# Moving the causal convolution and the gated input of a recurrent stage between three engines

## The chip, the cores and the metric

The kernel runs on one core of a Trainium2 chip. A core has a matrix engine (TensorE, PE in the rows), VectorE (DVE), ScalarE (ACT), GpSimd (POOL) and SyncE (SP), which here issues most of the DMA transfers. Each engine works through its own instruction stream in order; semaphores tie the streams together. The metric is the device time of one launch in microseconds; lower is better.

## The reference, cut to what matters

One step of a two-layer decoder: layer 0 is sparse attention, layer 1 a recurrent block (RG-LRU), and each is followed by a gated channel mixer. 256 prompt tokens and 8 sample tokens go through together, so a matrix multiply has 264 columns. The change lies in the recurrent block only:

```
gate, xb = split(a @ w_in)                       # 1024 channels each
xc = b + sum(xp[:, k:k + t] * w[k] for k in 0..3)  # xp: 3 kept rows, then xb
r  = sigmoid(block_diag(xc, w_ga) + b_ga)
ig = sigmoid(block_diag(xc, w_gx) + b_gx)
log_a = -8 * r * softplus(-lam);  a_t = exp(log_a)
b_t = sqrt(-expm1(2 * log_a)) * ig * xc
h_t = a_t * h_{t-1} + b_t                        # scan over the 256 tokens
y = (gelu(gate) * h) @ w_out
```

## The kernel before, in words

Activations are kept with channels on the 128 partitions and tokens along the free dimension, so 1024 channels are 8 chunks of 128x264. A matrix product is made of "units": 128 output channels, each from 8 chunks times three float16 matmuls (high times high, low activation times high, high times low weight; lines 1467, 1470, 1473). `hi` (ScalarE, line 595) and `lo` (VectorE, line 971) split a unit's weights into the two halves ahead of use.

The recurrent stage has 16 units, U_XB to U_XB+15: eight of `xb`, then eight of the gate branch. TensorE runs them in order and, after unit n+3, the two float32 gate products of chunk n (line 1797), for which it waits for the finished convolution `xc` (`xc_full`) and for the tanh of chunk n-2. Then it runs 20 small matmuls on ones (line 1479), and after that the first four output units together, chunk by chunk (lines 1614 to 1616), where each chunk c waits for the low half of y (`y_lo`, line 1376). All order is written out by hand in the loops over i = 0..15 that every engine has. In the kernel before, a chunk n of the stage takes these steps:

- VectorE, i = n: `xb` = result x reciprocal norm (line 1386; line 1388 for the gate branch). It waits for the TensorE unit.
- ScalarE: `tap3` = xb x w0 into a buffer of its own (line 923).
- GpSimd: the copy of the last rows of xb (line 1949), `xc` = xb x w3 + bias (line 1950), the sample columns' kept part `rpre` (line 1952), and `xc` += tap3 shifted by three (line 1954), which posts `xc_part`.
- VectorE, i = n+1 (`taps`): the shifts by one and by two (lines 1342 and 1345), then `xc_full`; then a `lo`.
- TensorE: gate products. ScalarE, i = n+4 (`keep_gates`): two tanh (line 841), a tanh and an exp (lines 844 and 846); it waits until the gated input of chunk n-2 has freed the buffer (`ix_done`).
- GpSimd, i = n+4: gated input `ix` = (tanh + 1) x xc, as an add (line 1959) and a product (line 1960), which posts `ix_done`.
- VectorE, i = n+5 (`b_part`): ix = (... + 1) x ix (line 1352).
- ScalarE takes the square root of four chunks at once (line 930, after chunks 3 and 7), GpSimd multiplies it in (`whole_b`, line 1943), VectorE scans (line 1362), GpSimd multiplies the Gelu by a row factor (line 1968), VectorE makes y (`mix`, line 1372), ScalarE its high half (lines 939 and 944), VectorE its low half (`mix_rest`, line 1376).

On GpSimd the loop interleaves `whole_b(n)` with the row factor of chunk n-4; on VectorE `scan(6)` and `scan(7)` stand after the low half of chunk 2.

Of the kernel before, what the change touches and what calls it, by code (L numbers as in the profile page):

```python
# [27 lines left out]
TP = 256  # L28
# [154 lines left out]
def build(nc, a, o):  # L183
    with ExitStack() as ctx:
# [148 lines left out]
        tap3 = z32  # L333
# [78 lines left out]
        tap3_done, xc_part, xc_full = sem("tap3_done"), sem("xc_part"), sem("xc_full")  # L412
# [169 lines left out]
        def _(act):  # L582
# [328 lines left out]
            for i in range(2 * DC):  # L911
# [7 lines left out]
                if i < DC:  # L919
                    act.wait_ge(acc_read, before(u) + 1)  # L920
                    if i >= 2:
                        act.wait_ge(xc_part, i - 1)
                    nc.scalar.activation(tap3[:, i % 2, :], xb[:, i % 2, :], ACT.Copy,
                                         scale=prm[:, ROW_CONV_W, i:i + 1]).then_inc(tap3_done, 1)
# [37 lines left out]
        def _(dve):  # L962
# [377 lines left out]
            def taps(n):  # L1340
                dve.wait_ge(xc_part, n + 1)
                steps.done(v.scalar_tensor_tensor(xc[:, n, 1:TP], xb[:, n % 2, 0:TP - 1], prm[:, ROW_CONV_W + 2, n:n + 1],
                                                  xc[:, n, 1:TP], ALU.mult, ALU.add))
                steps.wait()
                v.scalar_tensor_tensor(xc[:, n, 2:TP], xb[:, n % 2, 0:TP - 2], prm[:, ROW_CONV_W + 1, n:n + 1],
                                       xc[:, n, 2:TP], ALU.mult, ALU.add).then_inc(xc_full, 1)

            def b_part(n):

                dve.wait_ge(gate_ab, 2 * n + 2)  # L1350
# [27 lines left out]
            for i in range(2 * DC):  # L1378
# [4 lines left out]
                if i < DC:  # L1383
                    if i >= 2:
                        dve.wait_ge(xc_full, i - 1)
                    v.tensor_tensor(xb[:, i % 2, :], acc[:, u % 4, 0:T], rinv[:], ALU.mult).then_inc(acc_read, 1)
# [8 lines left out]
                if i >= 10:  # L1395
                    scan(i - 10)
                if i >= 14:
# [3 lines left out]
            for n in range(2, DC):  # L1401
                if n == 4:
                    scan(6)
                    scan(7)
# [410 lines left out]
        def _(pool):  # L1815
# [51 lines left out]
            def conv_params():  # L1867
# [4 lines left out]
                for k in range(3):  # L1872
                    w = prm[:, ROW_CONV_W + k:ROW_CONV_W + k + 1, :].to_broadcast([P, NS, DC])
                    small(g.tensor_tensor(rpre[:] if k == 0 else part, state[:, :, k, :], w, ALU.mult))
                    if k:
                        small(g.tensor_tensor(rpre[:], rpre[:], part, ALU.add))

# [67 lines left out]
            for i in range(DC + 4):  # L1945
                if i < DC:
# [3 lines left out]
                    small(g.tensor_scalar(xc[:, i, :], xb[:, p, :], prm[:, ROW_CONV_W + 3, i:i + 1],  # L1950
                                          prm[:, ROW_CONV_B, i:i + 1], ALU.mult, ALU.add))
                    small(g.tensor_tensor(xc[:, i, TP:T], xc[:, i, TP:T], rpre[:, :, i], ALU.add))
# [79 lines left out]
```

## Time and profile before

| what | us |
|---|---|
| median of 3 runs | 615.56 (615.41 to 616.15) |
| the profiled execution, its own time | 615.82 |
| its span, first to last instruction | 614.0 |
| TensorE busy in the span | 590.7 (96%) |
| VectorE, ScalarE, GpSimd busy | 457.2, 367.0, 238.6 |

The recurrent stage reaches from about 335 us to 405 us of the span. Times in the rows further down are microseconds from the start of the span; "idle before" is followed by the instruction that ended the idle time.

### The profile page before, as it was taken

To read this page: it belongs to the slowest core of one execution; us is meant where nothing else is said; L and a number is where in the kernel's file an instruction comes from. 1 tells how busy PE (TensorE), PEld (TensorE's weight loads), DVE (VectorE), ACT (ScalarE), POOL (GpSimd) and SP (SyncE) were. 2 spreads that over 40 slices of the span, in tenths; PEclk is the share of its full clock that TensorE was granted. 3 is DMA by queue.
4 is the path that set the end of the run, shared out by engine and by line. 5 is a ranking of instruction groups with operands and counts; after the bars stand their busy time and mean duration, and the time that the engine had idled before them with its cause. 6 is when DMAs were issued, how large, how long until landed. Compare 5 with 4: busy or idle time off the path is not lost.

```text
span 614.0 us, 12864 instructions
## 1 busy us (share of the span) xinstructions
PE 590.7 (96%) x5069; PEld 508.5 (83%) x5069; DVE 457.2 (74%) x897; ACT 367.0 (60%) x623; POOL 238.6 (39%) x259
## 2 busy tenths in 40 slices
PE   7899998999999999999999999798999999999995
PEld 7788886978888888888888778686888888888885
DVE  4788999456797778888677785978877777875432
ACT  6974556576666566565555688556656656653322
POOL 4232337733255445450000697823445545420000
PEclk9999998999999999999999999998999999999998
DMA  9949587319676667688996851054666666878501
GB/s 263 263 114 242 154 240 232 113 57 292 216 217 201 192 193 201 193 239 242 269 261 185 215 160 36 1 170 140 195 188 202 197 187 201 236 223 224 150 6 70
DMA packets 205421, 113.29 MB, mean 185 GB/s; under 512 B 5561, under 2 KB 202217, under 8 KB 205337
## 3 DMA queue, kind: packets, MB, share of 16 engines
q1 hardware_dynamic: 203169, 106.33, 61.4%
q0 software_dynamic: 1680, 5.79, 2.8%
q8 instruction: 40, 0.66, 0.4%
q10 hardware_dynamic: 512, 0.35, 0.2%
q14 instruction: 20, 0.16, 0.1%
HBM read 108.83 MB, written 3.86 MB: 184 GB/s over the span
## 4 chain that ended last, share of the span: by engine, by line
PE 70%; DVE 15%; POOL 6%; ACT 5%; issue 3%; DMA 1%; DVEq 0%; POOLq 0%; ACTq 0%
PE acc L1467 20%; PE acc L1470 20%; PE acc L1473 20%; DVE w_lo L971 5%; ACT w_hi L595 2%; POOL area L1954 1%; DVE area L1096 1%; PE acc L1614 1%; PE acc L1479 1%; DMA stage<-in_w_ffn_down 1%; PE acc L1616 1%; PE acc L1615 1%; POOL area L1950 1%; POOL area L1959 1%; POOL rtail L1949 1%
## 5 line engine op out<-in xcount | busy, mean ns | idle before, releaser
L1467 PE MATMUL acc<-aH,w_hi 128*128 128x264 f16 (+1 forms) x904 | 250.7, 277 | 1.7 <-DVE aL L980 1.6
L1470 PE MATMUL acc<-aL,w_hi 128*128 128x264 f16 (+1 forms) x904 | 250.6, 277 | 0.0
L1473 PE MATMUL acc<-aH,w_lo 128*128 128x264 f16 (+1 forms) x904 | 250.4, 277 | 0.0
L971 DVE SCALAR_TENSOR_TENSOR w_lo<-stage,w_hi 128x1024 f16<-128x1024 f32 (+1 forms) x155 | 204.0, 1320 | 33.6 <-ACT w_hi L595 33.2
L595 ACT ACTIVATE w_hi<-stage 128x1024 f16<-128x1024 f32 (+1 forms) x155 | 171.4, 1109 | 34.0 <-PE acc L1473 27.5
L1467 PE MATMUL acc<-zH,w_hi 128*128 128x264 f16 x384 | 106.0, 276 | 0.0
L1470 PE MATMUL acc<-zL,w_hi 128*128 128x264 f16 x384 | 106.0, 276 | 0.0
L1473 PE MATMUL acc<-zH,w_lo 128*128 128x264 f16 x384 | 106.0, 276 | 0.0
L1467 PEld LDWEIGHTS acc<-aH,w_hi 128*128 128x128 f16 (+1 forms) x904 | 89.0, 98 | 16.6 <-DVE aL L980 2.2
L1470 PEld LDWEIGHTS acc<-aL,w_hi 128*128 128x128 f16 (+1 forms) x904 | 90.3, 100 | 14.2 <-issue 0.3
L1473 PEld LDWEIGHTS acc<-aH,w_lo 128*128 128x128 f16 (+1 forms) x904 | 90.3, 100 | 13.3
L1899 POOL TENSOR_TENSOR scratch<-work,r0z 128x264 f32<-128x264 f32 x44 | 65.5, 1489 | 81.3 <-ACT work L865 81.3
L1897 POOL COPY ftail<-scratch 128x10 f32<-128x10 f32 x44 | 46.9, 1066 | 37.1 <-DVE scratch L1286 37.0
L860 ACT ACTIVATE work<-scratch,fprm 128x264 f32<-128x264 f32 x44 | 26.7, 607 | 54.1 <-DVE scratch L1286 54.0
L1286 DVE TENSOR_TENSOR scratch<-acc,rinv 128x264 f32<-128x264 f32 x44 | 19.0, 432 | 41.9 <-PE acc L1473 41.8
L1467 PEld LDWEIGHTS acc<-zH,w_hi 128*128 128x128 f16 x384 | 37.6, 98 | 5.7
L1473 PEld LDWEIGHTS acc<-zH,w_lo 128*128 128x128 f16 x384 | 37.6, 98 | 5.6
L1470 PEld LDWEIGHTS acc<-zL,w_hi 128*128 128x128 f16 x384 | 37.6, 98 | 5.5
L1833 POOL TENSOR_TENSOR sqsum<-sqsum,sq 128x264 f32<-128x264 f32 x21 | 16.5, 785 | 62.6 <-ACT sq L611 62.2
L865 ACT ACTIVATE work<-work 128x264 f32<-128x264 f32 x44 | 18.6, 423 | 35.0 <-DVE work L1297 34.9
L1910 POOL TENSOR_TENSOR area<-area,scratch 128x264 f32<-128x264 f32 x16 | 18.6, 1164 | 40.1 <-DVE area L1053 40.0
L604 ACT ACTIVATE aH<-hT,gcol 128x264 f16<-128x264 f32 x24 | 12.3, 514 | 32.5 <-DVE hT L1316 18.5
(407 smaller groups left out, 963.5 us busy)
## 6 DMA issues: line engine op xcount, KB each, us to landing
stage<-in_w_ffn_up SPq DMA_DIRECT2D x88, 512.0 KB, 4.0
stage<-in_w_ffn_down SPq DMA_DIRECT2D x32, 704.0 KB, 5.6
stage<-in_w_attn_in SPq DMA_DIRECT2D x22, 512.0 KB, 5.9
stage<-in_w_rec_in SPq DMA_DIRECT2D x16, 512.0 KB, 4.9
stage<-in_w_attn_out SPq DMA_DIRECT2D x8, 512.0 KB, 3.7
stage<-in_w_rec_out SPq DMA_DIRECT2D x8, 512.0 KB, 3.7
area<-in_w_attn_in SPq DMA_DIRECT2D x4, 512.0 KB, 5.5
area<-in_x_prompt SPq DMA_DIRECT2D x2, 512.0 KB, 4.8
```

Source lines behind the costliest of these rows:

```text
L595: nc.scalar.activation(halves_of(u)[0], stage[:, s, 0:n, 0:cols], ACT.Copy, scale=WSCALE).then_inc(hi_done, 1)
L860: nc.scalar.activation(c32[:, p, :], gs[:, p, :], ACT.Identity, scale=fprm[layer][:, FROW_W + 2, j:j + 1], bias=fprm[layer][:, FROW_B, j:j ...
L865: nc.scalar.activation(c32[:, p, :], c32[:, p, :], ACT.Gelu_apprx_tanh).then_inc(gelu_done, 1)
L971: v.scalar_tensor_tensor(low, stage[:, place_in_line(u) % 4, 0:n, 0:cols], WSCALE, high, ALU.mult, ALU.subtract).then_inc(lo_done, 1)
L1286: v.tensor_tensor(gs[:, p, :], acc[:, u % 4, 0:T], rinv[:], ALU.mult).then_inc(acc_read, 1)
L1467: t_.matmul(out, high[:, c, :], xH[:, x0 + c, :], start=first and c == 0, stop=False)
L1470: t_.matmul(out, high[:, c, :], xL[:, x0 + c, :], start=False, stop=False)
L1473: ins = t_.matmul(out, low[:, c, :], xH[:, x0 + c, :], start=False, stop=last and c == n - 1)
L1833: g.tensor_tensor(sqsum[:], sqsum[:], sq[:, c % 2, :], ALU.add).then_inc(ss_done, 1)
L1897: g.tensor_copy(ftail[:, :, j], gs[:, p, TP - 2:T]).then_inc(tail_copied, 1)
L1899: g.tensor_tensor(gr[:, p, :], c32[:, p, :], r0z[:], ALU.mult).then_inc(gr_done, 1)
L1910: g.tensor_tensor(dst, dst, rot[0:part, (before(u) + 1) % 2, :], ALU.subtract).then_inc(roped, 1)
```

## The change

The first convolution term goes to ScalarE: it writes xb x w3 + bias straight into `xc`, and the buffer `tap3` goes. VectorE makes all three shifted taps (shifts 1, 2 and 3) and the small add of the sample columns, and it also makes the gated input, in one instruction instead of two, at the head of `b_part`. GpSimd keeps the copy of the last rows, `whole_b` and the row factor. Before VectorE overwrites an xb buffer it now also waits for the GpSimd copy from it (`rt_copied`). Two orders change: all `whole_b` now come before all row factors on GpSimd, and on VectorE the scans 4 to 7 stand two and two in the last two rounds, ahead of the first and second `mix`. The file's line numbers move by a few.

```diff
-                    if i >= 2:
-                        act.wait_ge(xc_part, i - 1)
-                    nc.scalar.activation(tap3[:, i % 2, :], xb[:, i % 2, :], ACT.Copy,
-                                         scale=prm[:, ROW_CONV_W, i:i + 1]).then_inc(tap3_done, 1)
+                    nc.scalar.activation(xc[:, i, :], xb[:, i % 2, :], ACT.Identity, scale=prm[:, ROW_CONV_W + 3, i:i + 1],
+                                         bias=prm[:, ROW_CONV_B, i:i + 1]).then_inc(xc_part, 1)
...
             def taps(n):
                 dve.wait_ge(xc_part, n + 1)
-                steps.done(v.scalar_tensor_tensor(xc[:, n, 1:TP], xb[:, n % 2, 0:TP - 1], prm[:, ROW_CONV_W + 2, n:n + 1],
-                                                  xc[:, n, 1:TP], ALU.mult, ALU.add))
-                steps.wait()
-                v.scalar_tensor_tensor(xc[:, n, 2:TP], xb[:, n % 2, 0:TP - 2], prm[:, ROW_CONV_W + 1, n:n + 1],
-                                       xc[:, n, 2:TP], ALU.mult, ALU.add).then_inc(xc_full, 1)
+                if n == 0:
+                    dve.wait_ge(pre_done, 3)
+                for back in (1, 2):
+                    steps.done(v.scalar_tensor_tensor(xc[:, n, back:TP], xb[:, n % 2, 0:TP - back],
+                                                      prm[:, ROW_CONV_W + 3 - back, n:n + 1], xc[:, n, back:TP], ALU.mult, ALU.add))
+                    if back == 1:
+                        v.tensor_tensor(xc[:, n, TP:T], xc[:, n, TP:T], rpre[:, :, n], ALU.add)
+                    steps.wait()
+                v.scalar_tensor_tensor(xc[:, n, 3:TP], xb[:, n % 2, 0:TP - 3], prm[:, ROW_CONV_W, n:n + 1],
+                                       xc[:, n, 3:TP], ALU.mult, ALU.add).then_inc(xc_full, 1)
 
             def b_part(n):
 
+                dve.wait_ge(gate_tanh, 2 * n + 2)
+                v.scalar_tensor_tensor(ix[:, n, :], gates[:, n % 2, 1, :], 1.0, xc[:, n, :], ALU.add, ALU.mult).then_inc(ix_done, 1)
...
                     if i >= 2:
                         dve.wait_ge(xc_full, i - 1)
+                        dve.wait_ge(rt_copied, i - 1)
...
-                if i >= 10:
+                if 10 <= i < 14:
                     scan(i - 10)
+                if i >= 14:
+                    scan(2 * i - 24)
+                    scan(2 * i - 23)
...
             for n in range(2, DC):
-                if n == 4:
-                    scan(6)
-                    scan(7)
                 mix(n)
...
                     g.tensor_copy(rtail[:, :, i], xb[:, p, TP - 3:T]).then_inc(rt_copied, 1)
-                    small(g.tensor_scalar(xc[:, i, :], xb[:, p, :], prm[:, ROW_CONV_W + 3, i:i + 1],
-                                          prm[:, ROW_CONV_B, i:i + 1], ALU.mult, ALU.add))
-                    small(g.tensor_tensor(xc[:, i, TP:T], xc[:, i, TP:T], rpre[:, :, i], ALU.add))
-                    pool.wait_ge(tap3_done, i + 1)
-                    g.tensor_tensor(xc[:, i, 3:TP], xc[:, i, 3:TP], tap3[:, p, 0:TP - 3], ALU.add).then_inc(xc_part, 1)
-                if i >= 4:
-                    n = i - 4
-                    pool.wait_ge(gate_tanh, 2 * n + 2)
-                    pool.wait_ge(xc_full, n + 1)
-                    small(g.tensor_scalar(gates[:, n % 2, 1, :], gates[:, n % 2, 1, :], 1.0, None, ALU.add))
-                    g.tensor_tensor(ix[:, n, :], gates[:, n % 2, 1, :], xc[:, n, :], ALU.mult).then_inc(ix_done, 1)
                 if i >= 9:
                     whole_b(i - 9)
-            for n in range(3, DC + 4):
-                if n < DC:
-                    whole_b(n)
-                if n >= 4:
-                    pool.wait_ge(ggelu, 1 if n < 8 else 2 if n < 11 else 3)
-                    g.tensor_tensor(gateT[:, n - 4, :], gateT[:, n - 4, :], r0T[:], ALU.mult).then_inc(gr0_done, 1)
+            for n in range(3, DC):
+                whole_b(n)
+            for n in range(DC):
+                pool.wait_ge(ggelu, 1 if n < 4 else 2 if n < 7 else 3)
+                g.tensor_tensor(gateT[:, n, :], gateT[:, n, :], r0T[:], ALU.mult).then_inc(gr0_done, 1)
```

VectorE's row in the middle of the stage (i = 6), before; `area` holds xb, xc, ix and the gates, `prm` the weights, `ca` a unit's low weights:

```order
L1386 TENSOR_TENSOR area<-acc,rinv 128x264
L1342 SCALAR_TENSOR_TENSOR area<-area,prm 128x255
L1345 SCALAR_TENSOR_TENSOR area<-area,prm 128x254
L971 SCALAR_TENSOR_TENSOR ca<-stage,ca 128x1024
L1352 SCALAR_TENSOR_TENSOR area<-area 128x264
```

The same round in the changed kernel:

```order
L1391 TENSOR_TENSOR area<-acc,rinv 128x264
L1342 SCALAR_TENSOR_TENSOR area<-area,prm 128x255
L1345 TENSOR_TENSOR area<-area,rpre 128x8
L1342 SCALAR_TENSOR_TENSOR area<-area,prm 128x254
L1347 SCALAR_TENSOR_TENSOR area<-area,prm 128x253
L968 SCALAR_TENSOR_TENSOR ca<-stage,ca 128x1024
L1353 SCALAR_TENSOR_TENSOR area<-area 128x264
L1356 SCALAR_TENSOR_TENSOR area<-area 128x264
```

The round grows by three instructions: the small add, the tap by three, and the gated input.

GpSimd's last part of the stage before, where `area<-area` without r0T is `whole_b` or the gated input, and r0T is the row factor:

```order
L1959 TENSOR_SCALAR area<-area 128x264
L1960 TENSOR_TENSOR area<-area 128x264
L1943 TENSOR_TENSOR area<-area 128x264 x3
L1968 TENSOR_TENSOR area<-area,r0T 128x264
L1943 TENSOR_TENSOR area<-area 128x264
L1968 TENSOR_TENSOR area<-area,r0T 128x264
L1943 TENSOR_TENSOR area<-area 128x264
L1968 TENSOR_TENSOR area<-area,r0T 128x264
L1943 TENSOR_TENSOR area<-area 128x264
L1968 TENSOR_TENSOR area<-area,r0T 128x264 x5
```

And all that GpSimd does between the two sums of squares in the changed kernel:

```order
L1838 TENSOR_TENSOR sqsum<-sqsum,sq 128x264 x7
L1955 COPY rtail<-area 128x11 x8
L1949 TENSOR_TENSOR area<-area 128x264 x8
L1962 TENSOR_TENSOR area<-area,r0T 128x264 x8
L1964 COPY htail<-area 128x8x9
```

The eight `whole_b` now stand in a row ahead of the eight row factors, and the five instructions per chunk of convolution and gated input are gone.

## Rows read from the trace of the kernel before

**Rows 1.** The page, busy time (share of the span) and instructions of each engine.

```profile
PE 590.7 (96%) x5069; PEld 508.5 (83%) x5069; DVE 457.2 (74%) x897; ACT 367.0 (60%) x623; POOL 238.6 (39%) x259
```

**Rows 2.** Waits of TensorE, 342 to 405: total us, times, longest.

```profile
PE acc L1614 <- DVE zL L1376: 3.5, 4, 1.9
PE misc L1797 <- DVE area L1345: 0.7, 1, 0.7
```

**Rows 3.** Timeline of TensorE, 386 to 400: start, length, instruction, idle before it.

```profile
388.49 2.39 PE L1479 MATMUL misc<-ones 128*128 128x128 f32 x20
392.74 0.29 PE L1614 MATMUL acc<-zH 128*128 128x264 f16 x1 [1.85 <-DVE zL L1376]
...
398.99 0.29 PE L1614 MATMUL acc<-zH 128*128 128x264 f16 x1 [1.15 <-DVE zL L1376]
```

**Rows 4.** Timeline of VectorE, 355 to 368, same columns.

```profile
355.51 1.22 DVE L971 SCALAR_TENSOR_TENSOR zL<-stage,zH 128x1024 f16<-128x1024 f32 x1
356.65 0.42 DVE L1386 TENSOR_TENSOR area<-acc,rinv 128x264 f32<-128x264 f32 x1
...
360.35 0.42 DVE L1386 TENSOR_TENSOR area<-acc,rinv 128x264 f32<-128x264 f32 x1
361.89 0.62 DVE L1342 SCALAR_TENSOR_TENSOR area<-area,prm 128x255 f32<-128x255 f32 x1 [1.12 <-POOL area L1954]
362.55 0.48 DVE L1345 SCALAR_TENSOR_TENSOR area<-area,prm 128x254 f32<-128x254 f32 x1
...
365.00 0.42 DVE L1386 TENSOR_TENSOR area<-acc,rinv 128x264 f32<-128x264 f32 x1
```

**Rows 5.** Timeline of GpSimd, the gated input in the same stretch.

```profile
361.83 0.87 POOL L1959 TENSOR_SCALAR area<-area 128x264 f32<-128x264 f32 x1
362.79 0.86 POOL L1960 TENSOR_TENSOR area<-area 128x264 f32<-128x264 f32 x1
```

**Rows 6.** Timeline of VectorE in the channel mixer, 443 to 444.5.

```profile
442.92 0.48 DVE L1293 SCALAR_TENSOR_TENSOR work<-scratch,fprm,work 128x255 f32<-128x255 f32 x1
443.32 0.17 DVE L1295 TENSOR_TENSOR work<-work,fpre 128x8 f32<-128x8 f32 x1
443.44 0.48 DVE L1297 SCALAR_TENSOR_TENSOR work<-scratch,fprm,work 128x254 f32<-128x254 f32 x1
443.84 0.43 DVE L1272 TENSOR_TENSOR work<-acc,scratch 128x264 f32<-128x264 f32 x1
```

**Rows 7.** Timeline of ScalarE, 372 to 390.

```profile
373.01 0.85 ACT L841 ACTIVATE area<-misc,spl 128x264 f32<-128x264 f32 x2 [2.80 <-POOL area L1960]
...
383.43 1.08 ACT L930 ACTIVATE area<-area 128x1056 f32<-128x1056 f32 x1
```

**Rows 8.** Timeline of VectorE, 384 to 398.5.

```profile
387.84 1.15 DVE L1362 TENSOR_TENSOR_SCAN area<-area 128x256 f32<-128x256 f32 x1
...
394.39 0.97 DVE L1372 TENSOR_TENSOR work<-area 128x264 f32<-128x264 f32 x1
...
396.18 1.81 DVE L1362 TENSOR_TENSOR_SCAN area<-area 128x256 f32<-128x256 f32 x2
...
398.11 0.43 DVE L1372 TENSOR_TENSOR work<-area 128x264 f32<-128x264 f32 x1
```

**Rows 9.** Timeline of GpSimd, 384 to 398.5.

```profile
386.99 0.74 POOL L1968 TENSOR_TENSOR area<-area,r0T 128x264 f32<-128x264 f32 x1 [0.57 <-ACT area L933]
...
392.36 4.50 POOL L1968 TENSOR_TENSOR area<-area,r0T 128x264 f32<-128x264 f32 x5
```

**Rows 10.** Stretches: length, TensorE busy (instructions), granted clock, DMA share, GB/s.

```profile
375.00:385.00 10.00, 10.00 (x90) 1.00 0.01 2
390.00:394.00 4.00, 2.15 (x20) 1.00 0.00 0
418.00:422.00 4.00, 2.06 (x17) 1.00 0.57 167
422.00:426.00 4.00, 3.52 (x14) 0.57 0.61 177
```

More of the change, by code:

```diff
@@ L332, in build @@
         xb = area1[:, 7392:7392 + 2 * T].rearrange("p (b t) -> p b t", b=2)
-        tap3 = z32
         wordsH = zH[:, DC:FC, :].rearrange("p c t -> p (c t)")
@@ L411, in build @@
             sem(n) for n in ("lg_mm", "lg_max", "p_exp", "p_rcp", "p_norm", "p_turned", "p_kept", "o_mm", "o_hi", "o_lo"))
-        tap3_done, xc_part, xc_full = sem("tap3_done"), sem("xc_part"), sem("xc_full")
+        xc_part, xc_full = sem("xc_part"), sem("xc_full")
         gate_mm, gate_tanh, gate_ab, ix_done, bq_done, b_root, b_full, hs_done = (
@@ L1874, in conv_params @@
                     small(g.tensor_tensor(rpre[:] if k == 0 else part, state[:, :, k, :], w, ALU.mult))
-                    if k:
+                    if k == 1:
                         small(g.tensor_tensor(rpre[:], rpre[:], part, ALU.add))
+                g.tensor_tensor(rpre[:], rpre[:], part, ALU.add).then_inc(pre_done, 1)
             def ffn_params(layer):
```

## The prediction

> **What bounds the kernel now.** I read the page first, then TensorE's waits, then the timelines of the recurrent stage. TensorE is busy for 590.7 of 614.0 us [rows 1], so a change to the other engines can only win back TensorE's idle time, and here only that of the recurrent stage. The list of its waits there is short [rows 2]: 3.5 us in four waits for the low half of y, and 0.7 us in one wait for the convolution. The timeline shows where the 3.5 us sit [rows 3]. The sixteen units end at 388.49, twenty small matmuls follow, and the first matmul on y starts only at 392.74, after 1.85 us of idle time. The fourth y chunk starts at 398.99, again after waiting 1.15 us; between them stand two idle times of about 0.3. A y chunk is 12 matmuls; at 90 in 10.00 us [rows 10] that is 1.35 us of work, yet four chunks' starts lie 6.25 us apart instead of 4.05. From 398.99 on nothing waits. So **the start of the fourth y chunk sets the end**, and whatever moves it moves all that follows.
>
> What feeds y? In the middle of the stage VectorE's results come 4.65 us apart, 360.35 and 365.00 [rows 4], and within a round VectorE stands idle for 1.12 us until GpSimd's part of the convolution is there. GpSimd also makes the gated input in two instructions of 0.87 and 0.86 us [rows 5], and ScalarE's gates of chunk 5 start at 373.01 after waiting 2.80 us for it [rows 7]. The chain is thus: GpSimd, then ScalarE's gates and roots up to 384.51, then GpSimd's and VectorE's last steps, then TensorE.
>
> **Part 1, the middle of the stage.** GpSimd loses five instructions a chunk and keeps a copy; nobody waits for it there any more. VectorE's round becomes longer in work and loses its wait. The nearest rows for its new taps are those of the channel mixer, which has the same pattern without GpSimd beside it [rows 6]: the first tap takes 0.40 from start to start, the small add 0.12, a tap 0.40. Here the second tap is followed by one that waits for it, and such a handover costs 0.04 after the end instead of 0.08 before it (361.89 plus 0.62, next at 362.55 [rows 4]), so 0.52. Together 0.40 + 0.12 + 0.52 + 0.40 = 1.44. The result's own multiplication is 0.42 long [rows 4]; less the 0.08 by which neighbours overlap that is 0.35 from start to start. The weight split takes 1.14 (355.51 to 356.65). The gated input and the `b_part` after it are two more of 0.42 with a handover between: 0.35 + 0.52 = 0.87. A round is 0.35 + 1.44 + 1.14 + 0.87 = 3.80 us in place of 4.65.
>
> Result 5 comes at 356.65 now; up to there the new round has no gated input (2.93 us), which is TensorE's own pace or a little more, so I leave that time as it is. Result 8 is then at 356.65 + 3 x 3.80 = 368.05, and the gated input of chunk 3, for which ScalarE's gates of chunk 5 wait, is ready at 368.05 + 0.35 + 1.44 + 0.45 = 370.3. **That is 2.7 us before 373.01.** ScalarE's first term is an activation of the same size as the one it replaces and stays off this chain. Its queue behind is the same as before, so the second root ends 11.50 us after the gates of chunk 5 start (373.01 to 384.51 [rows 7]): 381.8. The new wait for GpSimd's copy costs nothing, since GpSimd has nothing queued ahead of it; behind it on VectorE stand all taps, and if the cover were gone, each round would grow by what the copy is late. TensorE's 0.7 us wait for the convolution mostly goes, though the gates' tanh then is next to be late; I count 0.5, so the sixteen units end at 388.0 and the fifteenth at 388.0 - 24 x 0.111 = 385.3.
>
> **Part 2, the end of the stage.** GpSimd has four `whole_b` and then the first row factor: five instructions of 0.74 alone and 0.90 (4.50 for five) against a busy VectorE [rows 9]. The first row factor is there between 385.5 and 386.3; before it was at 387.73. So it is no longer late, and **VectorE's own queue is next**. After the fifteenth unit it holds the result (0.35), a small product (0.4, an estimate from the 0.43 of the larger `mix`), scans 4 and 5, a `mix`, the last result, scans 6 and 7, a small add (0.2), a `mix` and the first low half. Against GpSimd a scan takes 1.07 from start to start (1.15 long), a `mix` 0.90 (0.97 long), where alone it takes 0.43; the pair of scans at the very end takes 1.74 (1.81) [rows 8]. All at the slow price: 385.3 + 0.35 + 0.4 + 2.14 + 0.9 + 0.35 + 1.74 + 0.2 + 0.9 + 0.9 = 393.2 for the first y chunk, 1.8 more, 395.0, for the second. But GpSimd's row factors 4 to 7 wait for a Gelu that stands behind the first y on ScalarE, so GpSimd rests for about 1 us, just while VectorE scans; and it is through by 394. That takes 0.4 to 0.8 off: the second y chunk starts at about 394.5. From there a chunk costs TensorE 1.35 and VectorE 0.9 to 1.8, once 0.1 late at most, and no scan stands in between any more. The fourth y chunk starts at 394.5 + 2.7 + 0.1 = 397.3 instead of 398.99.
>
> **The sum:** 398.99 - 397.3 = 1.7 us earlier. Against the profiled execution of 615.82 us (span 614.0) this is 614.1; the median of the runs shown, 615.56, lies 0.26 lower, so I forecast **613.9 us**. From here on 0.2%, or 1.2 us, is what a measurement can tell from no change: "faster" means below 614.3, "slower" above 616.8.
>
> **The bounds.** If GpSimd never got in VectorE's way, each of the nine contended steps would save 0.5, but TensorE's small matmuls (388.0 plus 2.39) hold the first chunk at 390.4 and the fourth at 394.5: 4.5 us earlier. That would need GpSimd to be done before 386, which the Gelu forbids; half of the way, 2.9 us, is the most I believe, 612.7. The other bound is the tap: among the taps of before are some of 0.62 instead of 0.48 [rows 4]. Three such a round make 0.45 more.
>
> **Rivals.** *VectorE becomes the pacing engine and the stage gets slower.* Its place is the rounds 0 to 7, its price what a round takes beyond 3.80. With all three taps at 0.62 and the GpSimd copy getting in between for 0.2, a round is 4.45, and the rounds before the fifth grow as well: result 8 comes 8 x 0.65 = 5.2 later, at 373.2, the gated input of chunk 3 2.4 us after 373.01, and with the new order giving back about 0.7 at the end the fourth chunk is 1.7 late: 617.3. It decides from a round of about 4.2 us on. For it speaks that VectorE gets all the work of a queue that is already 3.5 us long; against it that the slow taps stand beside a GpSimd instruction, and the same taps of the channel mixer are 0.48 throughout.
>
> *The end is given back to contention.* VectorE waits out each GpSimd instruction in full: 0.35 + 0.74 = 1.09 a step instead of 0.90, over nine steps 1.7 us, so 615.6: the gain is gone. The rows show 0.90 for VectorE and 0.90 for GpSimd in the same stretch [rows 8, 9], which is less than 1.09, so that only a part is blocked. The Trainium skill has such a rule on its page "SBUF — State Buffer", in "SBUF: two separate sides": a VectorE instruction with two SBUF inputs and a GpSimd instruction that reads SBUF share one port pair, and the one that comes second is blocked until the first is finished altogether. By that rule the time would be this rival's, 615.6; the trace here agrees that they block each other and does not agree on the whole length.
>
> *The clock falls at the joint.* From 418 to 422 TensorE was busy for 2.06 of 4 us, and in the next 4 us the mean granted clock was 0.57, mostly the lower level, 1.2 GHz, in place of 2.4; it ran 14 instructions where 36 fit [rows 10]; by the clock's share, 0.43 of 4 us, 1.7 us were lost. From 390 to 394 it was busy for 2.15 of 4 us and the clock stayed. In the changed kernel its idle time before y is in one piece, 390.4 to 393. If the clock falls there, 1.7 to 2 us go: 615.8. The opposite is as open: that the dip after 422, which no step of this sum touches, is not there after the shift, giving 612.2.
>
> **Chances and range.** The forecast 0.50, spread from 612.7 to 615.1, of which 0.36 lies below 614.3; the missing dip or a deeper gain 0.10; contention in full 0.13; the clock at the joint 0.14; VectorE as pacing engine 0.13. Faster is 0.36 + 0.10 = 0.46, within 0.2% is 0.14 + 0.13 + 0.14 = 0.41, slower 0.13. The range takes in the dip at 612.2 and goes up to 616.9, which leaves out most of the slow rival. TensorE does the same work in all cases, and no DMA is moved.
>
> **What would show it.** VectorE's results in rounds 5 to 8 3.8 us apart, with no idle time behind GpSimd; taps of 0.48; ScalarE's gates of chunk 5 at 370 and the second root ending at 382; the first row factor done by 386.5; the first y chunk at 392.6 to 393.2, only one long idle time on TensorE before it, and the fourth near 397.3. I would be wrong first in the round: if it is over 4.2 us, there is no gain. Second in the queue after the fifteenth unit: if the first y chunk starts after 394.3, the order of the scans has eaten what the middle won.

## The result and the profile after

| what | before, us | changed, us |
|---|---|---|
| median of 8 runs each, side by side | 615.31 (613.17 to 616.15) | 610.93 (610.26 to 612.69) |
| profiled execution, its own time | 615.82 | 612.69 |
| its span | 614.0 | 610.6 |

The ratio, estimated from all executions of both, is 0.9945, 95% interval 0.9931 to 0.9959: by it the changed kernel is 3.4 us faster, where 1.7 was forecast. (The two medians lie 4.4 apart and the two means 3.6; eight executions of each leave that much open.) The median of 610.93 is outside the range of 612.2 to 616.9. The sign was right, the size was not.

The lines of the changed kernel that answer to those of before follow. The page, busy time, for [rows 1]; GpSimd gave up 31 us and VectorE took 2:

```profile
PE 588.4 (96%) x5069; PEld 508.0 (83%) x5069; DVE 459.5 (75%) x921; ACT 367.8 (60%) x623; POOL 207.2 (34%) x219
```

Waits of TensorE between 342 and 405 for [rows 2]; the wait of 0.7 on the convolution is gone, and so is one of 0.19 on the tanh (its row stands further down), and of four on y one is left:

```profile
PE acc L1619 <- DVE zL L1380: 2.1, 1, 2.1
```

Timeline of TensorE (start, length, instruction, idle before) for [rows 3]:

```profile
386.99 2.39 PE L1484 MATMUL misc<-ones 128*128 128x128 f32 x20
391.52 0.40 PE L1619 MATMUL acc<-zH 128*128 128x264 f16 x1 [2.14 <-DVE zL L1380]
```

Timeline of VectorE in the rounds, for [rows 4] and [rows 6]. Results (L1391, L1393) come 3.79 us apart, 359.32, 363.11, 366.90, with no idle time in between, and the three taps are 0.47 or 0.48 long, none 0.62 (the first and the third of one round stand here):

```profile
359.32 0.42 DVE L1391 TENSOR_TENSOR area<-acc,rinv 128x264 f32<-128x264 f32 x1
359.66 0.47 DVE L1342 SCALAR_TENSOR_TENSOR area<-area,prm 128x255 f32<-128x255 f32 x1
...
360.69 0.48 DVE L1347 SCALAR_TENSOR_TENSOR area<-area,prm 128x253 f32<-128x253 f32 x1
...
363.11 0.43 DVE L1391 TENSOR_TENSOR area<-acc,rinv 128x264 f32<-128x264 f32 x1
```

```profile
369.19 0.85 ACT L840 ACTIVATE area<-misc,spl 128x264 f32<-128x264 f32 x2 [0.81 <-DVE area L1353]
...
379.62 1.09 ACT L927 ACTIVATE area<-area 128x1056 f32<-128x1056 f32 x1
```

The last two are ScalarE's gates of chunk 5 and its second root, for [rows 7].

The end of the stage, VectorE (for [rows 8]) and then GpSimd (for [rows 9]):

```profile
384.49 0.43 DVE L1393 TENSOR_TENSOR area<-acc,rinv 128x264 f32<-128x264 f32 x1 [1.08 <-PE acc L1478]
384.84 0.70 DVE L1365 TENSOR_TENSOR rtmp<-area,prm 128x32 f32<-128x32 f32 x1
385.57 2.23 DVE L1366 TENSOR_TENSOR_SCAN area<-area 128x256 f32<-128x256 f32 x2
387.72 0.40 DVE L1376 TENSOR_TENSOR work<-area 128x264 f32<-128x264 f32 x1
...
388.39 1.26 DVE L1366 TENSOR_TENSOR_SCAN area<-area 128x256 f32<-128x256 f32 x2
...
390.15 0.42 DVE L1376 TENSOR_TENSOR work<-area 128x264 f32<-128x264 f32 x1
390.50 0.97 DVE L1380 TENSOR_TENSOR zL<-work,zH 128x264 f16<-128x264 f32 x1
```

```profile
380.78 3.28 POOL L1949 TENSOR_TENSOR area<-area 128x264 f32<-128x264 f32 x4 [3.85 <-ACT area L927]
384.02 3.23 POOL L1962 TENSOR_TENSOR area<-area,r0T 128x264 f32<-128x264 f32 x4
389.41 3.54 POOL L1962 TENSOR_TENSOR area<-area,r0T 128x264 f32<-128x264 f32 x4 [2.16 <-ACT area L934]
```

Stretches of TensorE (length, busy and instructions, granted clock, DMA share, GB/s) for [rows 10]. The clock falls to the lower level, 1.2 GHz, right after the idle time before y; the dip that before has from 422 to 426 is not there:

```profile
390.00:392.00 2.00, 0.48 (x3) 0.88 0.00 0
392.00:394.00 2.00, 2.00 (x11) 0.50 0.04 8
394.00:396.00 2.00, 2.00 (x16) 0.76 0.00 0
...
424.00:428.00 4.00, 4.00 (x38) 1.00 0.70 202
```

Such dips have to be kept apart from the change. Over a whole execution the mean granted clock is 0.997 in the best ones, and each dip takes 0.003 of it: the profiled execution of before was at 0.991, that of the changed kernel at 0.994. One dip costs 1.7 to 1.8 us in whole executions: on the chip where the changed kernel was run a second time, 11 executions of before at 0.996 to 0.998 took 613.4 on average and 19 at 0.994 or 0.995 took 615.2. (A dip is a stretch of about 4 us in which the granted clock falls to its lower level; an execution without one, at 0.996 or above, is called undipped.) At equal clock that chip gives:

| mean granted clock | before (executions) | changed (executions) | difference |
|---|---|---|---|
| 0.996 to 0.998 | 613.4 (11) | 610.75 (5) | -2.7 |
| 0.994 to 0.995 | 615.2 (19) | 612.4 (6) | -2.8 |

**The change itself is worth about 2.75 us.** The rest of the 3.4 is then which executions fell into which group; the clocks of the first eight executions of before are not known, so for that first comparison this is an inference.

### The profile page after: what moved, and what is told of

Same layout as the page of the kernel before. It is cut to its first block, busy times and chain, and to the rows that moved or that the text cites. A ratio compares the mean times of both kernels' runs of the same rounds, so it can differ in the third digit from the quotient of the medians.

```text
span 610.6 us, 12826 instructions
## 1 busy us (share of the span) xinstructions
PE 588.4 (96%) x5069; PEld 508.0 (83%) x5069; DVE 459.5 (75%) x921; ACT 367.8 (60%) x623; POOL 207.2 (34%) x219
## 4 chain that ended last, share of the span: by engine, by line
PE 74%; DVE 15%; ACT 3%; issue 3%; DMA 2%; POOL 2%; DVEq 0%; POOLq 0%; ACTq 0%
PE acc L1472 21%; PE acc L1475 21%; PE acc L1478 21%; DVE w_lo L968 6%; DMA stage<-in_w_ffn_down 2%; ACT w_hi L594 2%; PE acc L1619 1%; PE acc L1621 1%; PE acc L1620 1%; DVE area L1093 1%; PE misc L1802 1%; PE acc L1484 1%; POOL sqsum L1838 1%; DVE area L968 1%; PE misc L1577 1%
```

## The experiments

In all of them I compare one more set of numbers, worked out from the timelines and counted from the start of the stage's RECIPROCAL on VectorE, so that what happens ahead of the stage drops out: where the small matmuls on ones begin (the units' end), where the first y chunk starts, and where the first output block is read by VectorE. "Clock at the joint" is the granted clock around the first y chunk in the one profiled execution of each, not that of its other executions. For before and changed the rows the numbers are taken from, beside 388.49 and 392.74 in [rows 3], are these:

```profile
340.81 1.80 DVE L985 RECIPROCAL rinv<-root 128x264 f32<-128x264 f32 x1 [0.48 <-ACT root L615]
```

```profile
404.94 0.43 DVE L1247 SCALAR_TENSOR_TENSOR hT<-acc,hT 128x264 f32<-128x264 f32 x1 [1.48 <-PE acc L1616]
```

```profile
340.58 1.80 DVE L982 RECIPROCAL rinv<-root 128x264 f32<-128x264 f32 x1 [0.48 <-ACT root L614]
```

```profile
403.17 0.43 DVE L1244 SCALAR_TENSOR_TENSOR hT<-acc,hT 128x264 f32<-128x264 f32 x1 [3.36 <-PE acc L1621]
```

| kernel | units end | first y | first output | clock at the joint | whole runs, ratio to before |
|---|---|---|---|---|---|
| before | 47.68 | 51.93 | 64.13 | 1.00 | 1 |
| changed | 46.41 | 50.94 | 62.59 | falls | 0.9945 |
| changed again | 46.42 | 50.94 | 62.68 | falls | 0.9956 |
| e1, orders only | 47.72 | 54.74 | 67.50 | falls | 1.0042 |
| e2, engines only | 46.41 | 49.76 | 60.86 | 1.00 | 0.9947 |
| e3, convolution only | 46.89 | 51.43 | 63.27 | falls | 0.9971 |
| e12, gated input only | 47.28 | 51.82 | 62.25 | 1.00 | 0.9974 |
| e4, longer warm | 46.40 | 50.94 | 61.38 | 1.00 | 0.9972 |
| e6, one tap more | 48.48 | 53.35 | 63.78 | 1.00 | 0.9995 |
| e7, two taps more | 50.83 | 56.11 | 67.77 | falls | 1.0037 |
| e8, old scan order | 46.40 | 48.63 | 60.28 | 1.00 | 0.9940 |
| e9, scans early | 46.40 | 48.63 | 60.70 | 1.00 | 0.9985 |
| e10, e9 and 3 warm | 46.40 | 47.68 | 62.43 | falls | 0.9988 |
| e11, small row factor | 46.41 | 49.07 | 59.07 | 1.00 | 0.9929 |

**The changed kernel once more** (no edit), 12 executions on another chip.

> The changed kernel itself, once more, on one chip with the others and with the clock of every run of both kernels beside its time. If the 3.4 us came from the chain alone, it is 3.4 us faster than before among runs of the same mean granted clock too. If part of it is that fewer of its executions have a stretch at the lower clock, then at an equal mean clock (0.997 to 0.998) the gap is 2 to 2.5 us, and the rest is the share of runs at 0.994 and below.

611.87 against 614.87, ratio 0.9956 (0.9938 to 0.9973). The stage is the same to 0.1 us, the dip at the joint included (0.57 from 392 to 396). So the stage repeats; how many executions are undipped does not: 6 of 8 the first time, 5 of 12 now.

**e1, the two orders alone**, on the kernel before:

```diff
-                if i >= 10:
+                if 10 <= i < 14:
                     scan(i - 10)
+                if i >= 14:
+                    scan(2 * i - 24)
+                    scan(2 * i - 23)
...
-                if n == 4:
-                    scan(6)
-                    scan(7)
```

and GpSimd's two loops as in the change. **e2, the engines alone**, is the other half: the changed kernel with both of these orders put back.

> The kernel before with only the two changes of order (scans 4 to 7 two and two in the last rounds on VectorE, all whole_b before the row factors on GpSimd); convolution and gated input stay where they were. If the gain of 3.4 us sits in the order at the end, this alone is 2 to 3.4 us faster (612 to 613). If it sits in the middle of the stage, this is no faster and rather slower: the first row factor then comes behind four whole_b that start after 384.5, at about 388 instead of 387, and the scans stand in front of the second mix; worked out with the durations of before, the first y chunk starts near 395 instead of 392.7 and the fourth near 399.8 instead of 399.0, so 615.3 + 0.8 = about 616.

> The changed kernel with both orders of before put back (scan i-10 in each round, scans 6 and 7 behind the low half of chunk 2, whole_b and row factor interleaved). If the gain comes from the work moved off GpSimd in the middle, this keeps all of it: result 8 and the second root at the same times as in the changed kernel, first y chunk earlier (about 390) because only two scans stand before it, the fourth at 395.5 to 396.5; as fast as the changed kernel or up to 0.8 us faster (611 to 612 against 615.3). If the order of the scans is what brings it, 1 us or more of the 3.4 us is lost (over 613).

e1 took 616.54, ratio 1.0042 (1.0028 to 1.0057); e2 611.27, 0.9947 (0.9927 to 0.9966). TensorE's row of e1, and what its clock does behind it:

```profile
394.52 0.40 PE L1614 MATMUL acc<-zH 128*128 128x264 f16 x1 [4.63 <-DVE zL L1376]
```

```profile
396.00:400.00 4.00, 4.00 (x21) 0.50 0.01 4
```

With the square roots still late, four scans instead of two ahead of the first low half, and a first row factor behind four `whole_b`, make the first y chunk 2.8 us later, and the clock stays at its lower level through 400. **The two orders are worth nothing by themselves; all of the gain is the engines'.** At a clock of 0.994 e2 is 3.2 us under before (611.6 against 614.8), more than the whole change at an equal clock (two chips, though, and e2 had four such executions).

**e3 and e12, the two moves apart** (both with the new orders). e3 leaves the gated input on GpSimd:

```diff
             def b_part(n):
-                dve.wait_ge(gate_tanh, 2 * n + 2)
-                v.scalar_tensor_tensor(ix[:, n, :], gates[:, n % 2, 1, :], 1.0, xc[:, n, :], ALU.add, ALU.mult).then_inc(ix_done, 1)
...
+                    small(g.tensor_scalar(gates[:, n % 2, 1, :], gates[:, n % 2, 1, :], 1.0, None, ALU.add))
+                    g.tensor_tensor(ix[:, n, :], gates[:, n % 2, 1, :], xc[:, n, :], ALU.mult).then_inc(ix_done, 1)
```

e12 keeps these on VectorE and takes the convolution as before, with the first two lines of its GpSimd part:

```diff
+                    small(g.tensor_scalar(xc[:, i, :], xb[:, p, :], prm[:, ROW_CONV_W + 3, i:i + 1],
+                                          prm[:, ROW_CONV_B, i:i + 1], ALU.mult, ALU.add))
```

> The changed kernel with the gated input left on GpSimd in its two instructions (add 1, multiply), in the round i = n + 4 after the copy of the last rows; VectorE has the three taps but not the gated input. If it was the convolution on GpSimd that paced the stage, nearly all of the gain stays (611 to 612.5): GpSimd's round is 0.2 + 0.9 + 0.85 = 2 us, below TensorE's 3.6. If the gated input was the costly part, half or more of 3.4 us goes (over 613). Contention between GpSimd's product and VectorE's taps should show as single taps of 0.6 to 0.9 us.

> The complement of the run that moved the convolution alone: the convolution as in the kernel before (three operations on GpSimd, two taps on VectorE), the gated input on VectorE, both orders new. GpSimd's round loses 0.87 of its 3.6 to 3.7 us and VectorE's gains about 0.9 and stays under 3.8. If the gain of the changed kernel comes mostly from taking work off GpSimd, whichever work, this gives 611.0 to 612.5, near the 612.35 of the other half. If the shorter chain of the convolution is needed for it (ScalarE's term against three GpSimd operations), the two conv waits stay and the time stays at 613.5 to 615.

e3: 612.35, 0.9971 (0.9955 to 0.9987). e12: 612.88, 0.9974 (0.9961 to 0.9988). TensorE's waits of e3 and then of e12:

```profile
PE acc L1617 <- DVE zL L1378: 2.3, 2, 2.1
PE misc L1800 <- DVE area L1347: 0.2, 1, 0.2
```

```profile
PE acc L1616 <- DVE zL L1378: 2.4, 2, 2.1
PE misc L1799 <- DVE area L1345: 0.7, 1, 0.7
```

The expectations don't quite meet this: e3's median lies where "nearly all of the gain stays" was written, but its ratio keeps 1.8 of 3.4 us, and e12's median falls between its two cases (its expectation also took GpSimd's round at 3.6 to 3.7 us, where [rows 4] have 4.65). Each half wins 1.6 to 2.4 us at equal clock, together 2.75: each alone takes so much off GpSimd that the roots come sooner. e12 keeps the 0.7 wait of TensorE for the convolution, but its units end 0.4 sooner than before's; e3 cuts that wait to 0.2. ScalarE's second root starts 42.62 after the stage's start in before, 38.37 in e3, 39.90 in e12 and 39.04 in the changed kernel. So e3 brings the roots forward by 4.25 us, more than both moves together (3.58), and e12 by 2.72. The two halves do not add up, and after either TensorE's long wait at the end is for VectorE's low half of y, 2.1 us, as in the changed kernel.

**e6 and e7, a longer round.** One or two taps more per chunk, into a buffer nobody reads (e7 has the line twice):

```diff
+                v.scalar_tensor_tensor(z32[:, 0, 3:TP], xb[:, n % 2, 0:TP - 3], prm[:, ROW_CONV_W, n:n + 1],
+                                       xb[:, n % 2, 0:TP - 3], ALU.mult, ALU.add)
```

> The changed kernel with one more tap-sized instruction on VectorE in each of the eight rounds (its result goes to an unused buffer): a round of 4.2 us instead of 3.8. If VectorE's round is what now paces the middle of the stage, as the prediction's sum has it, the gates of chunk 5 come some 3 us later and close to all of the gain is gone (about 613 to 615); 4.2 us was named as the point of no gain. If VectorE has slack there, the time stays that of the changed kernel.

> The changed kernel with two more tap-sized instructions on VectorE in each of the eight rounds: a round of 4.6 us. If VectorE paces the middle, this is slower than the kernel before, by 2 to 4 us (617 to 619), and twice as far from the changed kernel as one more tap, or more. If it has slack, at most 1 us is lost.

e6: 614.70, 0.9995 (0.9980 to 1.0009). e7: 616.77, 1.0037 (1.0022 to 1.0052). VectorE's results in the rounds of e6, and TensorE's waits in e6 and e7:

```profile
358.23 0.43 DVE L1393 TENSOR_TENSOR area<-acc,rinv 128x264 f32<-128x264 f32 x1
...
362.41 0.42 DVE L1393 TENSOR_TENSOR area<-acc,rinv 128x264 f32<-128x264 f32 x1
```

```profile
PE misc L1804 <- ACT area L840: 1.3, 2, 1.0
```

```profile
PE misc L1806 <- ACT area L840: 3.6, 3, 2.2
```

Rounds of 4.18 us give the time of before (at equal clock 0 to 0.5 us under it). Rounds of 4.57 (362.24 to 366.81) give a median 1.9 longer, 1.5 at equal clock (616.7 of 6 against 615.2 of 19); that is slower, but less than the 617 to 619 expected. The point from which the slow rival decides, 4.2 us, was right, and so was its mechanism: the later gated input delays the gates' tanh, and TensorE waits for that. The table shows how the two sides cancel: in e6 the units end 0.8 us later than in before, but the way from there to the first output is 1.15 us shorter (15.30 instead of 16.45).

**e4, the warm matmuls over the idle time**: are 19 pairs enough to keep the clock up at the joint?

```diff
-            keep_warm(A[:, 0:P], 10)
+            keep_warm(A[:, 0:P], 19)
```

> The changed kernel with 19 instead of 10 of the two-pass matmuls on ones ahead of the first y chunk; they fill the idle time of 2.1 us before it (9 more at 0.24 us). If the clock at the joint (0.50 for some 3.5 us around 392 in the profiled run) fell because TensorE stood idle there, it stays at 1.00 in this one and the fastest runs come more often; the median falls by up to 1.7 us. If the fall is not bound to that idle time, the time is that of the changed kernel (0.9945 of before) and the granted clock still falls somewhere in 390 to 425 in some runs.

612.47, 0.9972 (0.9955 to 0.9989), no gain over the changed kernel. The clock holds at the joint in the profiled execution (first output 61.38 instead of 62.59), but it dips from 104 to 108:

```profile
104.00:108.00 4.00, 3.59 (x19) 0.58 0.47 160
392.00:396.00 4.00, 3.60 (x32) 1.00 0.00 0
```

That the longer matmuls are what held it is not shown: in e12 the clock held as well, with 2.14 us of idle time at the same place. At equal clock the times are those of the changed kernel (610.8 against 610.75, on two chips). So a dip at the joint costs 1.2 us there, and an execution without one there can have one elsewhere. The run also shows the stage without a dip: the first output is 64.13 - 61.38 = 2.75 us sooner than before, the same number as the equal-clock table.

**e8, VectorE's old scan order** with GpSimd's new one:

```diff
-                if 10 <= i < 14:
+                if i >= 10:
                     scan(i - 10)
-                if i >= 14:
-                    scan(2 * i - 24)
-                    scan(2 * i - 23)
...
+                if n == 4:
+                    scan(6)
+                    scan(7)
```

> The changed kernel with VectorE's scans in the order of before (one a round, scans 6 and 7 behind the low half of chunk 2), while GpSimd keeps the new order. With two scans fewer ahead of it the first y chunk should start near 390.2 instead of 391.5 and the fourth near 395.5; about 1 us faster than the changed kernel at an equal clock if the scans of the last two rounds are what holds the first y chunk. If it is the row factor that holds it, nothing changes here, and the gain of the kernel with both old orders came from GpSimd's interleaving.

610.87, 0.9940 (0.9919 to 0.9961); the changed kernel beside it 611.87. The first y chunk starts right behind the warm matmuls, and the waits lie between later ones (one of 0.26 at 393.51 stands between these two):

```profile
391.72 0.29 PE L1619 MATMUL acc<-zH 128*128 128x264 f16 x1 [0.27 <-DVE zL L1380]
...
395.63 0.29 PE L1619 MATMUL acc<-zH 128*128 128x264 f16 x1 [0.60 <-DVE zL L1380]
```

At equal clock it is 0.8 us under the changed kernel (undipped: 610.0 of 2 against 610.75 of 5; at 0.994 to 0.995: 611.3 of 5 against 612.4 of 6, 1.1). The intervals of the two ratios overlap, and two undipped executions are few. **With e2 it is the fastest version here that computes everything** (e2 undipped: 609.8 of 2, before on its chip 613.2 of 14; both are 3.4 under before): the new scan order seems to cost 0.8 to 1.1 us, and GpSimd's new order is worth nothing that shows.

**e9 and e10, a VectorE order of my own** (scan 4 already in round 13, the first low half in 14), e10 also with `keep_warm` 3 instead of 10; the lines they replace are left out here:

```diff
+                if i == 13:
+                    scan(4)
+                if i == 14:
+                    mix(0)
+                    scan(5)
...
+                    scan(6)
+                if i == 15:
+                    mix(1)
+                    scan(7)
```

> The changed kernel with VectorE's last units written in another order, so that its chain begins with unit 13: scan 4 in unit 13; mix 0, scan 5, rest 0, scan 6 in unit 14; mix 1, scan 7 in unit 15. If the time still lost at the end of the stage is VectorE's order (old scan order: chunk 0 starts 2.2 us after the first warm matmul and is followed by waits), then chunk 0 starts right behind the ten warm matmuls (48.6 us after the stage's RECIPROCAL), at most one wait follows, the first output block comes at 58.7 to 59.8 against 61.4 to 62.6 in the changed kernel, and the run is 2 to 3 us under the changed kernel at the same clock (608 to 609). If GpSimd's row factors are what ends last instead, chunk 0 keeps 50.9 and the time stays at 611.

> As the last one, with 3 warm matmuls instead of 10. Seven of them less are 1.7 us (each 0.24). If nothing but the warm matmuls holds chunk 0 there, it starts at 47.0 to 47.6 and the run gains up to 1.5 us more (607). If VectorE's chain is as long, it starts at about 48.2 and the gain is 0 to 0.5. If the clock falls in the longer gap, the window after the gap shows about 0.5, and the run is 1.2 to 1.7 us slower than the last one instead.

Neither brought the expected gain: 613.54, 0.9985 (0.9968 to 1.0001), and 613.32, 0.9988 (0.9972 to 1.0003). The first y chunk is as early as foretold, and the gain is given back by the second. In order: e9's second y chunk, two of its scans on VectorE, and e10's clock at the joint:

```profile
392.27 0.29 PE L1622 MATMUL acc<-zH 128*128 128x264 f16 x1 [1.90 <-DVE zL L1380]
```

```profile
383.80 1.14 DVE L1366 TENSOR_TENSOR_SCAN area<-area 128x256 f32<-128x256 f32 x1
...
389.66 1.23 DVE L1366 TENSOR_TENSOR_SCAN area<-area 128x256 f32<-128x256 f32 x1
```

```profile
394.00:396.00 2.00, 2.00 (x11) 0.50 0.00 0
```

All four scans now stand beside GpSimd's row factors (383.66 to 390.35 without a pause), 1.14 to 1.23 long each; in the changed kernel scans 6 and 7 fall into GpSimd's rest and take 1.26 for the two. The order moved the waiting and added contention. And the clock: only one execution of the 24 was undipped (609.86 us, e9), and 19 of the 24 were at 0.992 or below. That is where most of the median's loss lies: at 0.994 e9 took 612.3 (2 executions) against 615.1 for before on its chip, 2.8 less, which is what the changed kernel gains. As far as two executions tell, the order is then not slower in itself; it lost the expected further gain to contention and the rest to a clock that these runs do not explain.

**e11, GpSimd's row factor on 8 columns** of 264; the other 256 are left without it, so this part of the computation is missing:

```diff
-                g.tensor_tensor(gateT[:, n, :], gateT[:, n, :], r0T[:], ALU.mult).then_inc(gr0_done, 1)
+                g.tensor_tensor(gateT[:, n, 0:8], gateT[:, n, 0:8], r0T[:, 0:8], ALU.mult).then_inc(gr0_done, 1)
```

> The changed kernel with GpSimd's row factor on 8 of its 264 columns (the others are left without the factor, so that part of the computation is missing). GpSimd is then nearly idle while VectorE scans and mixes. If the fast scans and mixes there are lengthened by GpSimd's row factors (contention), the scans that took 2.23 us for two come back to about 1.8 and chunk 0 starts 0.5 to 1.5 us sooner (49.4 to 50.4 after the stage's start; run 609.5 to 610.5). If VectorE's chain alone sets chunk 0 and contention is worth nothing, it stays at 50.9 and the time within 0.3 us of the changed kernel.

610.16, 0.9929 (0.9912 to 0.9946), the fastest of all. VectorE's end of the stage, to lay beside that of the changed kernel:

```profile
385.48 0.20 DVE L1365 TENSOR_TENSOR rtmp<-area,prm 128x32 f32<-128x32 f32 x1
385.72 1.27 DVE L1366 TENSOR_TENSOR_SCAN area<-area 128x256 f32<-128x256 f32 x2
...
389.81 0.42 DVE L1380 TENSOR_TENSOR zL<-work,zH 128x264 f16<-128x264 f32 x1
```

```profile
PE acc L1619 <- DVE zL L1380: 0.3, 1, 0.3
```

The small product takes 0.20 instead of 0.70, the pair of scans 1.27 instead of 2.23, the low half 0.42 instead of 0.97, and nothing on VectorE there waits for GpSimd in either kernel. The first y chunk starts 1.87 us sooner, and the first output 61.38 - 59.07 = 2.3 (e4 as the undipped changed kernel). **Contention with GpSimd is what the end of the stage still pays, some 2 us of it.** This is a price, not a version.

## Why the forecast was short

Two terms were wrong. In the sum, what TensorE's waits in the units cost was put at 0.5 us and measured 1.27. Outside the sum, the base of 615.56 stood at the level of executions with a dip, and the changed kernel's median at that of executions without one, about 1.9 us. The prediction had each as a case by itself, the deeper gain (612.7) and the missing dip (612.2), and no case for both at once; together they put the median below the range.

**The middle of the stage: right in the round, wrong in what TensorE's waits cost.** The round was 3.79 us for a forecast of 3.80; results at 352.62 and 355.53 show 2.91 for the rounds without a gated input, forecast 2.93. ScalarE's gates of chunk 5 start at 369.19 for a forecast of 370.3, and the second root ends at 380.71 for 381.8; of the 1.1 us, 0.23 is the stage's earlier start. The other 0.9 was there at result 5 already: 14.95 after the stage's start (355.53) where I had left it at 15.84 (356.65). "I leave that time as it is" took these rounds for TensorE's pace, and they were not. Before, VectorE waits 1.29 us for GpSimd's part of the convolution in the first of them, and result 2 comes 7.28 after the stage's start; in the changed kernel that wait is gone and result 2 comes at 6.23. Three rows, two of before and one of changed:

```profile
345.84 0.48 DVE L1342 SCALAR_TENSOR_TENSOR area<-area,prm 128x255 f32<-128x255 f32 x1 [1.29 <-POOL area L1954]
...
348.09 0.42 DVE L1386 TENSOR_TENSOR area<-acc,rinv 128x264 f32<-128x264 f32 x1
```

```profile
346.81 0.42 DVE L1391 TENSOR_TENSOR area<-acc,rinv 128x264 f32<-128x264 f32 x1
```

What failed is the step "I count 0.5" for TensorE's waits, which puts the units' end at 388.0. The waits listed 0.66 and 0.19 of idle time, but read from start to start they cost more. TensorE in the kernel before, around the first of them:

```profile
354.72 0.28 PE L1473 MATMUL acc<-aH,area 128*128 128x264 f16 x1
355.65 1.13 PE L1797 MATMUL misc<-area,scratch 128*128 128x264 f32 x4 [0.66 <-DVE area L1345]
356.62 0.28 PE L1467 MATMUL acc<-aH,area 128*128 128x264 f16 x1
```

```profile
351.13 0.28 PE L1473 MATMUL acc<-aH,area 128*128 128x264 f16 x1
351.24 1.05 PE L1797 MATMUL misc<-area,scratch 128*128 128x264 f32 x4
352.13 0.28 PE L1467 MATMUL acc<-aH,area 128*128 128x264 f16 x1
```

```profile
366.85 1.13 PE L1797 MATMUL misc<-area,scratch 128*128 128x264 f32 x4 [0.19 <-ACT area L841]
```

Without a wait the gate matmuls start 0.11 after their predecessor and the next unit 0.89 after them (351.13, 351.24, 352.13). With the wait it is 0.93 and 0.97: together 0.90 lost, where the row says 0.66. The gate matmuls follow each other 3.59 apart without a wait (359.32, 362.91); the wait for the tanh, 0.19 in the row of 366.85, put them 3.94 apart and the next ones (370.51) 3.66, 0.42 lost. Both are gone, less 0.05 that one start in the changed kernel still loses: 1.27 us in all, and the units end 47.68 - 46.41 = 1.27 sooner. I counted 0.5, so this term was 0.77 short.

**The end of the stage: right in kind, 0.3 short.** From the stage's start, the second y chunk was forecast at 394.5 - 340.81 = 53.7 and the fourth at 397.3 - 340.81 = 56.5; the undipped stage of e4 has them at 52.7 and 55.4 (394.75 and 397.46, less 342.02). Of the 1.05 us between, 0.77 came with the units' end, 0.3 from contention that was shorter than counted, all terms taken together. From start to start, the forecast's slow prices held where GpSimd was at work (two scans 2.15 for 2.14, low half 0.89 for 0.90), and the small product (0.73 for 0.4) and the small add (0.58 for 0.2) were slower; but the two `mix` (0.33 and 0.35 for 0.9 each) and the second pair of scans (1.18 for 1.74) cost less. The first `mix` and that pair fell into GpSimd's rest from 387.2 to 389.4, 2.16 us long where I had counted about 1. That the row factors would no longer be late, and VectorE's own queue be next, was right. I also counted on the new orders ("no scan stands in between any more"); e1 and e8 show that they bring nothing, or cost something.

**The rest is the clock of the base.** Both steps make 1.7 into 2.75. From 615.56 that gives 612.8, inside the range. The median measured is 610.93 because six of the changed kernel's eight executions were at 0.997, while 615.56 is the level of before with a dip in it (615.2; undipped 613.4), and the profiled one, at 0.991, had two. I took a base with dips in it and let the chances of a dip only enter as rivals. That part of the number is luck, not mechanism: whether the change makes dips rarer these runs can't tell, with 36 of 90 executions of before, on three chips, at 0.996 or above, and 11 of 20 of the changed kernel.

**The rivals.** *VectorE as the pacing engine*: not the case at 3.79 us; e6 confirms its turning point and e7 that it is slower beyond. *Contention in full*: not in full. A scan beside GpSimd adds 0.48 (2.23 against 1.27 for two) to its own time, a low half 0.55, and GpSimd's instructions take 0.81 each (3.23 for four) instead of 0.74. The Trainium skill's rule on its page "SBUF — State Buffer", in "SBUF: two separate sides", blocks the second instruction until the first is finished altogether, which would add up to 0.74 here. The trace agrees that the two hold each other up, and e11 shows that GpSimd's instructions are what does it; of the size it shows two thirds to three quarters. *The clock at the joint*: it did fall there, in the profiled executions of the changed kernel, and cost 1.2 us (62.59 against 61.38), not the 1.7 to 2 that I gave it; at the same time the dip after 422 was missing: of the 3.4 us by which the span is shorter, 1.8 are there at the first output (404.94 to 403.17) and 1.6 come after it. Both cases happened, and they about cancel in the profile.

## What to carry to other kernels

Price a wait of TensorE from the starts on both of its sides, against the same place without a wait, not from its row of idle time; here the rows said 0.85 and the starts 1.32. And see whether a round that looks paced by one engine is only late from a wait further ahead. Here GpSimd stood in the chain, and moving its work to an engine with idle gaps was worth more than the orders tried around it; the turning point (here a round of 4.2 us) could be worked out from the rows beforehand. Before a difference of a few us is ascribed to a change, compare executions of the same mean granted clock, since one short dip here is over half as large as the change, and let a range hold the cases together as well as one by one.

## What the runs showed that I had not expected

- A dip of TensorE's clock, about 4 us at a mean of 0.57 to 0.6, costs 1.2 us to 1.8 us, at the joint and in the averages of whole executions; it comes in varying places (92 to 100, 104 to 108, 392 to 400, 416 to 428) in executions of nearly the same kernel. Its price depends on the place: before has one at 92 to 100, and its recurrent stage starts only 0.23 us later than that of the changed kernel, which has none ahead of it. Taking the idle time away at one of them, as e4 did, did not make undipped executions more frequent (4 of 12).
- Undipped executions are rarer in some kernels than in others, and long idle times at the joint may be why; it was seen afterwards, and not tested. The kernels with the longest idle time there (e1 4.6 us, e7 2.9, e6 2.5, e10 2.4) and e9 (1.9, behind a single chunk) had 3 undipped executions in 60, against 25 in 77 for the others and 36 in 90 for before. The group was made after the fact, and doesn't split cleanly: the changed kernel, e3 and e12, with 2.1 us, count among the others. What decides between a dip and none in one execution stays open: with 2.14 us of idle time the clock fell in the changed kernel and held in e12, and in e6 it held with 2.5.
- Shortening one chain under contention can lengthen it: e9 put four scans beside GpSimd where the changed kernel has two, and its first output came no sooner than with the old scan order of e8 (60.70 and 60.28).
